# The second matrix of both MLPs by seven block products, in a pass of its own through DRAM

## The reference

```
def squared_relu_mlp(x, w1, w2):
    return jnp.square(jax.nn.relu(x @ w1)) @ w2
```

## Time and profile before

| | us |
|---|---|
| median of three runs | 5415.53 |
| fastest run | 5411.13 |
| span of the profiled execution (core 5, the slowest of 8: 5385.8 to 5402.6) | 5402.6 |
| PE busy in it | 5231.8 |
| DVE, ACT, POOL busy | 2641.7, 1955.8, 751.2 |

### The profile page before, as it was taken

One profiled execution on the slowest core, in us unless ns is written; L12 is line 12 of the kernel. 1 busy time (PEld: TensorE's weight loads), 2 busy tenths in 40 slices (PEclk: granted clock), 3 DMA queues, 4 the chain that ended last, 5 costly groups with the idle time before them and its releaser, 6 DMA issues.

```text
span 5402.6 us, 80099 instructions; the slowest of 8 cores (5385.8 to 5402.6 us)
## 1 busy us (share of the span) xinstructions
PE 5231.8 (97%) x27646; PEld 2542.2 (47%) x27646; DVE 2641.7 (49%) x4779; ACT 1955.8 (36%) x3529; POOL 751.2 (14%) x1206
## 2 busy tenths in 40 slices
PE   8999999999999989999999999999999999999997
PEld 3444444444444434444656555444444444444446
DVE  3645556665333743433554444476634337433337
ACT  3434432333222342132444555323421235223224
POOL 1111110000000300001312222000000013000013
PEclk9999999999999999999999999999999999999999
DMA  9333559876544685455642332568864557645443
GB/s 165 58 56 52 84 102 182 187 166 135 94 72 80 139 195 85 71 84 86 112 111 55 66 67 60 117 161 183 174 118 71 86 85 153 150 80 92 73 84 91
DMA packets 358732, 578.04 MB, mean 107 GB/s; under 512 B 127808, under 2 KB 197312, under 8 KB 358208
## 3 DMA queue, kind: packets, MB, share of 16 engines
q0 software_dynamic: 102816, 340.90, 40.0%
q1 hardware_dynamic: 255520, 232.02, 15.4%
HBM read 789.12 MB, written 99.61 MB: 165 GB/s over the span
## 4 chain that ended last, share of the span: by engine, by line
PE 84%; DMA 8%; DVE 3%; issue 2%; SPq 1%; ACT 1%; POOL 0%; DVEq 0%; ACTq 0%; POOLq 0%
PE bank L427 81%; DMA t<-z 4%; DVE t L443 2%; PE bank L1602 2%; DMA z<-t 1%; ACT t L440 1%; DMA x2b<-t 1%; DVE t L446 1%; DMA t<-xq 1%; SPq L230 1%; DMA t<-w2l 1%; DMA hgD<-t 1%; SPq L240 0%; DMA t<-w 0%; DMA x<-t 0%
## 5 line engine op out<-in xcount | busy, mean ns | idle before, releaser
L427 PE MATMUL bank<-t,t 128*128 128x512 bf16 (+3 forms) x25438 | 5133.6, 364 | 147.9 <-DVE t L443 51.8
L427 PEld LDWEIGHTS bank<-t,t 128*128 128x128 bf16 x25438 | 2406.5, 99 | 2793.4 <-issue 359.9
L443 DVE TENSOR_TENSOR t<-t,bank 128x512 f32<-128x512 f32 x1024 | 699.0, 686 | 1498.0 <-PE bank L427 1491.6
L440 ACT ACTIVATE t<-bank 128x512 f32<-128x512 f32 (+5 forms) x1396 | 718.4, 555 | 1707.7 <-PE bank L427 1689.3
L440 ACT ACTIVATE t<-t 128x512 f32<-128x512 f32 (+3 forms) x1208 | 747.1, 623 | 890.8 <-DVE t L443 693.1
L443 DVE TENSOR_TENSOR t<-t,t 128x512 f32<-128x512 f32 (+6 forms) x1428 | 901.1, 668 | 176.4 <-ACT t L440 76.2
L230 POOL DMA_DIRECT2D t<-w x416 | 219.8, 530 | 2503.7 <-PE bank L427 2369.3
L440 ACT ACTIVATE t<-t,t 128x512 bf16<-128x512 f32 (+5 forms) x525 | 333.6, 669 | 488.7 <-DVE t L443 355.5
L443 POOL TENSOR_TENSOR t<-t,t 128x512 f32<-128x512 f32 (+2 forms) x276 | 328.3, 1202 | 458.0 <-DVE t L443 268.9
L446 DVE SCALAR_TENSOR_TENSOR t<-t,t,t 128x512 f32<-128x512 f32 (+2 forms) x428 | 301.4, 728 | 132.1 <-DMA t<-z 77.7
L440 ACT ACTIVATE t<-bank,t 128x256 bf16<-128x256 f32 (+2 forms) x332 | 174.5, 566 | 218.2 <-PE bank L427 109.5
(11 more groups left out here) (38 smaller groups left out, 350.1 us busy)
## 6 DMA issues: line engine op xcount, KB each, us to landing
t<-w POOLq DMA_DIRECT2D x416, 512.0 KB, 7.5
t<-z SPq DMA_DIRECT2D x192, 256.0 KB, 6.1
t<-w2l POOLq DMA_DIRECT2D x116, 384.0 KB, 6.2
z<-t SPq DMA_DIRECT2D x128, 256.0 KB, 6.3
t<-w_out POOLq DMA_DIRECT2D x51, 512.0 KB, 8.7
t<-xq SPq DMA_DIRECT2D x64, 256.0 KB, 5.5
x<-t SPq DMA_DIRECT2D x64, 256.0 KB, 6.3
t<-x SPq DMA_DIRECT2D x64, 256.0 KB, 3.8
```

The costliest lines, as they stand in the source:

```text
L427: fns = [lambda e, o=o, l=l, r=r, a=a, b=b: e.matmul(out=o, lhsT=l, rhs=r, start=a, stop=b, **kw) for (o, l, r, a, b) in items]
L440: return self.P.op("act", lambda e: e.activation(out=out, in_=in_, func=func, **kw), c_act(n, bias is not None and scale is not None), **k)
L443: return self.P.op(eng, lambda e: e.tensor_tensor(out=out, in0=a, in1=b, op=op), c_pool(n) if eng == "pool" else c_dve(n, rate), **k)
```

## The change

- **Two passes.** `phase_w1` makes all hidden tiles of a layer, in 32 groups for each half, and stores them in DRAM (`hD`, 0.5 MB for each group). The order is groups 0 to 13 of half 0, then 14 to 31 of both halves with the same weights, then 0 to 13 of half 1; so w1 is read 46/32 times instead of twice. x16 and T of half 1 stand in SBUF as well, in what was the accumulators' arena (`"xB"`), and `phase_out` now stores z of s = 0, 1 in DRAM, too.
- **The second matrix by seven products.** A `Chunk` is a quarter q (16 row blocks) of the hidden features of one half: 8 loads of 0.5 MB from `hD`, and 8 DVE subtractions of 128x2048 in `Chunk.part`. `group2` multiplies it with two row blocks of outputs at a time, 8 groups of 7 products for each chunk, 7 chunks in each layer: 56 groups. The eighth (half 1, q = 3) is multiplied plainly, in four parts of 256 columns, with 16 row blocks where it was 12.
- **Its additions.** Of the seven results of a group five are added by DVE from PSUM straight into z; two (`side`) are copied by ACT into a tile of the arena `"t"` (room for two) and added into z by POOL. The products on X wait for the addition before them.
- **z.** `init` loads z from DRAM in pairs of row blocks and applies the residual's gain and bias with ACT, two groups ahead. Three of eight pairs of half 0 are stored and loaded again for LayerNorm (`ln_item`).
- **w2 in bf16.** `convert` casts w2 from DRAM to DRAM, 32 DMAs of 2 MB float32 to 1 MB bf16 for each layer, on POOL's queue: two after each `o_proj` of `phase_m` for layer 0, one after every fourth item beside attention for layer 1. The second matrix is then loaded as bf16 by SP, 128 transfers of 0.5 MB a layer.
- **LayerNorm.** The second operation of `norm_tile` and the sum of squares in `stat2` go to POOL for s = 2, 3 of `phase_out`, and so does the second operation for half 0 of the MLPs.

Counted in the built programs: matmuls of 512 columns 21564 before, 20412 after (1152 fewer); of 256 columns 2792 and 3304 (512 more).

```diff
             v_proj(p, wv, j, vv)
             o_proj(p, wo, j, so)
+            convert(k, 0, 8 * p + 2 * j, 2)
             scan(p, j, qk, vv, so, kk)
...
+def convert(k, layer, i, n):
+
+
+    after = [o for o in k.P.ops[-40:] if o.eng == "pe"][-1:]
+    for i in range(i, min(i + n, 32)):
+        j = (i // 8, i % 8)
+        k.conv[(layer,) + j] = k.P.dma("pool", k.d["w2c_%d" % layer][j], k.d["w2_%d" % layer][j], 1 << 20, extra=after)
...
+def products(k, ws_, W, last, X, banks, after, free=None):
...
+    plan = (("X", lo, 0, "B11", None), ("Z", lo, 1, "B21", ("raw", 0)), ("X", sa, 0, "T2", None), ("Y", sa, 1, "T1", ("S", 0)),
+            ("X", sb, 0, "T3", None), ("Y", sb, 1, "B22", ("S", 1)), ("X", hi, 1, "T4", ("raw", 1)))
+    for i, (bn, w, j, o, drop) in enumerate(plan):
+        first = bn not in bank
+        if first:
+            bank[bn] = P.ps(banks)
+        b, (ts, x) = bank[bn], X[o]
+        g = k.mm([(b[:], w[:, j, kp * 128:kp * 128 + 128], x(kp), first and kp == 0, kp == 7) for kp in range(8)], 8 * c_mm(512),
+                 more=not first, reads=[w] + ts, **({"writes": [b]} if first else {"rw": [b]}))
...
+        after(i, b, g)
+        if i in (1, 5, 6):
+            P.free(b)
+        paced(k, g)
...
+        stored[(pr, n)] = P.store(k.d["hD"][pr, n // 8, n % 8 // 4, :, :, n % 4].rearrange("o p t -> p o t"), hq[:], 1 << 19, reads=[hq])
...
+class Chunk:
...
+        for o in (0, 1, 3, 2):
+            for half in range(2):
+                t = self.R[(o, half)] = P.sb(2048, F16, [4, 512], ar="ops", al=True)
+                P.dma("sp", t[:], k.d["hD"][blk, q, half, o], 1 << 19, writes=[t], extra=[stored[(blk, 8 * q + 4 * half + i)] for i in range(4)])
...
+    def sub(self, o, a, b, h, **kw):
+        self.k.tt("dve", o[:], a[:], b[:], ALU.subtract, 2048, rate=2.0, **kw)
...
+    NA = 14
+    order = [(n, 0) for n in range(NA)] + [(n, p) for n in range(NA, 32) for p in range(2)] + [(n, 1) for n in range(NA)]
...
+    def init(blk, n):
+
+        for s in (2 * blk, 2 * blk + 1):
+            while k.later and not P.room(1024, F32, "acc"):
+                paced(k, None)
...
+    def group2(blk, q, n, cur, nxt):
...
+        def add(z, b):
+            k.tt("dve", z[:], z[:], b[:], ALU.add, 512, reads=[b], rw=[z])
+
+        def side(z, b):
+            t = P.sb(512, ar="t")
+            k.act(t[:], b[:], AF.Copy, 512, reads=[b], writes=[t])
+            k.tt("pool", z[:], z[:], t[:], ALU.add, 512, reads=[t], rw=[z])
             P.free(t)
...
+        def after(i, b, g):
+            if i == 1:
+                side(C[(0, 0)], b)
+            elif i == 3:
+                side(C[(1, 1)], b)
+            else:
+                add(C[{0: (0, 0), 2: (0, 1), 4: (1, 1), 5: (0, 1), 6: (1, 0)}[i]], b)
...
+    for blk, q in steps[:-1]:
+        cur = nxt
+        at = steps.index((blk, q)) + 1
+        nxt = Chunk(k, *steps[at], stored)
...
+            its = [f for i, it in enumerate(its) for f in ([it] if i % 4 else [it, lambda: convert(self.k, 1, len(self.k.conv) - 32, 1)])]
```

More of the change, by code:

```diff
@@ L938, in norm @@
             return
-        o = P.half(("x16", s), ar="x" if s < 2 else None, dt=F16)
+        ar = "x" if s < 2 else "xB"
+        o = P.half(("x16", s), ar=ar, dt=F16)
         if s < 2:
@@ L1027, in __init__ @@
         self.todo = []
-        for i, (name, idx, shape, sums) in enumerate(reqs):
+        for i in range(len(reqs)):
             self.todo += [(i, "raw", 0), (i, "raw", 1)]
-            if i and reqs[i - 1][3]:
+            if i:
                 self.todo += [(i - 1, "S", 0), (i - 1, "S", 1)]
-        if sums:
-            self.todo += [(i, "S", 0), (i, "S", 1)]
+        self.todo += [(i, "S", 0), (i, "S", 1)]
         self.ts = {}
@@ L1040, in pump @@
             i, kind, part = self.todo[0]
-            name, idx, shape, sums = self.reqs[i]
-            t = k.unit([shape[0] // 2, shape[1]], F16, until is not None)
+            t = k.unit([2, 1024], F16, until is not None)
             if t is None:
@@ new lines, in products @@
+def products(k, ws_, W, last, X, banks, after, free=None):
+    P = k.P
+    lo, hi, sa, sb = W
+    bank = {}
+    plan = (("X", lo, 0, "B11", None), ("Z", lo, 1, "B21", ("raw", 0)), ("X", sa, 0, "T2", None), ("Y", sa, 1, "T1", ("S", 0)),
[7 more added lines that the diff above has]
+                 more=not first, reads=[w] + ts, **({"writes": [b]} if first else {"rw": [b]}))
+        if drop and last:
+            ws_.drop(*drop)
+        if free:
+            free(o)
+        after(i, b, g)
+        if i in (1, 5, 6):
+            P.free(b)
+        paced(k, g)
@@ L1110, in late, with w1_ops, phase_w1 @@
+def w1_ops(x, s):
+    d = {"B11": [x[(kp, s)] for kp in range(8)], "B21": [x[(kp + 8, s)] for kp in range(8)], "B22": [x[(kp + 8, s + 1)] for kp in range(8)]}
+    for i in range(4):
+        d["T%d" % (i + 1)] = [x[("T", i, kp, s)] for kp in range(8)]
+    return {o: (ts, lambda kp, ts=ts: ts[kp][:]) for o, ts in d.items()}
+def phase_w1(k, layer, x16, ws_, order):
+    P = k.P
+    PB = [0, 1, 2, 3, 4, 5]
+    stored = {}
+    def late(*a, **kw):
         P.bias += 30
-        eng(*a, **kw)
+        k.act(*a, **kw)
@@ L1112, in late @@
         P.bias -= 30
-    def group1(h, har, n, x, ss, pops):
-        s0, s1 = ss
-        (lo, hi, sa, sb), drop = ws_.get(), ws_.drop
-        def prod(b, first, W, j, X):
-            g = k.mm([(b[:], W[:, j, kp * 128:kp * 128 + 128], X(kp)[:], first and kp == 0, kp == 7) for kp in range(8)], 8 * c_mm(512),
-                     more=not first, reads=[W] + [X(kp) for kp in range(8)], **({"writes": [b]} if first else {"rw": [b]}))
-            if pops:
-                paced(k, g)
-        def T(j):
-            return lambda kp: x[("T", j, kp)]
+    X = {0: w1_ops(x16, 0)}
@@ new lines, in phase_w1, with done @@
+    for at, (n, pr) in enumerate(order):
+        if at == 0 or order[at - 1][0] != n:
+            W = ws_.get()
+        if at == len(order) - 8:
+            (a, b), (d, e) = P.arena["w0"]
+            P.arena["w"] = [(a, b), (d, e - 8192 // GR)]
+        last = at + 1 == len(order) or order[at + 1][0] != n
+        if pr not in X:
+            while k.later:
+                paced(k, None)
+            X[pr] = w1_ops(x16, 2 * pr)
+        hq = P.sb(2048, F16, [4, 512], ar="h")
+        c = {}
+        def done(t, i, relu=True):
+            if relu:
+                late(t[:], t[:], AF.Relu, 512, rw=[t])
+            late(hq[:, i], t[:], AF.Square, 512, reads=[t], par=[hq])
+            P.free(t)
@@ new lines, in after @@
+        def after(i, b, g):
+            if i == 0:
+                c[0] = copy(b)
+            elif i == 1:
+                k.tt("dve", c[0][:], c[0][:], b[:], ALU.add, 512, reads=[b], rw=[c[0]])
+                done(c[0], 0)
+            elif i == 2:
+                c[1] = copy(b)
+            elif i == 3:
+                c[3] = copy(b)
+            elif i == 4:
+                k.tt("dve", c[3][:], c[3][:], b[:], ALU.add, 512, reads=[b], rw=[c[3]])
+                done(c[3], 3)
+            elif i == 5:
+                k.tt("dve", c[1][:], c[1][:], b[:], ALU.add, 512, reads=[b], rw=[c[1]])
+                done(c[1], 1)
+            else:
+                done(copy(b, AF.Relu), 2, False)
@@ new lines, in arena_w2 @@
+def arena_w2(k):
+    P = k.P
+    P.close()
+    n = 4096 // GR
+    w = P.arena["w0"]
+    acc = P.arena["acc"]
+    taken = {g for lo, hi in w + acc for g in range(lo, hi)}
+    ops = [g for g in range(P.low, P.ngr - n + 1, n) if not any(g + i in taken for i in range(n))][:22]
+    assert len(ops) == 22
+    taken |= {g + i for g in ops for i in range(n)}
+    (a, b), (c, d) = w
+    rest = [(d - 2 * n, d)]
+    for g in range(P.low, P.ngr):
+        if g not in taken:
+            if rest[-1][1] == g:
+                rest[-1] = (rest[-1][0], g + 1)
+            else:
+                rest.append((g, g + 1))
+    P.arena = {"w": [(a, b), (c, d - 2 * n)], "w0": w, "acc": acc, "ops": [(g, g + n) for g in ops], None: rest[1:] + [(d - n, d)], "t": [(d - 2 * n, d - n)]}
```

414 lines of the change are left out of this document (201 added, 213 removed).

## The result

The kernel before took 5410.32, 5411.13 and 5415.53 us and the changed kernel 5517.95, 5550.22 and 5554.55: a ratio of **1.024, interval 1.018 to 1.030**. Forecast were 5252 us (0.970) in a range of 5200 to 5325. In many executions the four cores of one die run at a lower clock for a time: all times and ratios here leave those executions out, and where a trace holds such a die, the other die's cores are read.

The account below looks back on a forecast made before the run. PE was taken as the bound (5231.8 of 5402.6 us busy); -192 - 28 + 11 + 6 + 20 + 8 + 6 + 6 = -163 gave a 5240 us span, plus 12.9 to the median: 5252 us, range 5200 to 5325.

Parts of the forecast that it names:

- PE's loads there are prefetched: phase_m and attention: casts delay no PE loads, only their issue holds POOL; +6 us, bounds 0 and 35.
- Rival 2: DMA: conversions hold up kD, hgD or weight loads and each MLP's front saturates; +64 us, 5316, chance 0.10.
- Additions of the second matrix: Second pass: DVE and side additions free banks nearly in time; 0.1 us for each of 112 groups, +11, bounds 0 and 56.
- rival 1: Second pass: POOL's side additions pace it, 0.7 us overrun in each of 112 groups; +67 us, 5319, chance 0.15.
- LayerNorm of half 0 beside the second matrix: Second pass: POOL's LayerNorm operations delay side additions in most of 13 groups, 10 us a layer; +20, bounds 0 and 45.
- Differences: Between chunks: 128x2048 DVE subtractions of 1.09 us delay additions, some twice a turn, 12 turns; +6, bounds 0 and 17.
- switch: From first pass to second: z loads wait for slots that x of half 1 frees late; +8, bounds 0 and 24.
- phase_out and the first groups: There more z and hD traffic brings the DMA share from 0.87 to about 1; +6, bounds 0 and 25.
- PE busy near 5040: Sign in the profile after, whole kernel; the prediction is wrong if PE busy falls by less than 185 us.
- removed matmuls are removed time: PE, full in the MLPs' steady stretches: fewer matmuls save 248.8 us, added ones cost 56.6, net -192.
- no gap above 5 us at the turn of halves: Sign in the profile after: PE has no gap above 5 us where the MLP's halves meet.
- the old turn: Between MLP halves: PE gaps of 22.3 and 6.1 us vanish, as x no longer comes from DRAM there; -28.

Follow-up runs that it names:

- experiment 1: The kernel before with the 64 DRAM to DRAM casts added at the change's places, their output unused: 5599.06 us.
- experiment 2: The change without the 64 casts, w2 read as float32 and cast in its load: 5361.86 to 5367.4 us, ratio 0.993 to the kernel before.
- experiment 6: The change with all seven additions of a second-pass group on DVE: ratio to the kernel before 1.012 with the casts, 0.979 (5286.79 and 5294.4 us) without.
- experiment 5: The change with all 64 casts moved into the first pass of the MLP that reads them: 5530.13 and 5530.53 us, ratio 1.024 to the kernel before.
- experiment 8, first kernel: The change without casts, second-pass additions, every LayerNorm's second operation and phase_out's statistics on DVE: 5307.16 and 5309.47 us, ratio 0.983 to the kernel before.

## Why the prediction was wrong

- **The step that failed: "PE's loads there are prefetched", +6 (0 to 35) for the casts.** They cost 168 to 195 us (experiments 1, 2, 6), and as much in the first pass (experiment 5). My price of a cast was right (6.4 us of the DMA engines predicted, 6.1 measured), and so was the share of 0.62 in the attention; in `phase_m` it was 0.65 where I had 0.75. I took "the engines have spare share" for "nothing waits", and looked at loads with a distance. What stands between one PE instruction and the next there is a store and a transpose (`kD`, `hgD`, `oD`; 2.7 us to landing in the median for `oD`); beside casts the worst take 27 to 80 us, and SP's own queue stops at them. Why a store or a transpose gets so late, no run here shows. Rival 2 named this, at +64: the mechanism right, its size 2.6 times too small, since I took the upper ends of terms of which the one for the casts was bounded by POOL's issue time (0.54 us each).
- The Trainium skill, DMA: Bandwidth & Descriptors, section Queues, rings and completion order, says that each DMA engine takes turns between queues by packet. By that rule a small store waits for one long piece at each turn, and shorter rows help. The runs agree in part: rows of a tenth the length gave 46 of 195 us back without the change and 77 of 168 with it; what holds up the attention's stores at short rows no run here settles.
- **"Additions of the second matrix", +11.** Taken off POOL they gave 63 and 72 us. That is rival 1 near its price (+67), with the sign that it named: gaps released by DVE, and DVE by POOL. The overrun was not one of every group, as the rival had it: those with statistics did not gain from the move (experiment 6). I set the rival too low (0.15) by a weak comparison: the two rows of POOL that differ by 8% have different output types, and DVE was busy in only half of both stretches (114.24 of 220 us, 76.42 of 160). The rule of the Trainium skill, SBUF — State Buffer, section Who interferes with whom, that a DVE instruction with two SBUF inputs and a POOL instruction that reads SBUF exclude each other, fits what was measured: 1282 against 685 ns, and 678 against 683 with one input in PSUM. From 2150 to 2250 us of the change POOL's addition took 1538 ns, and DVE's of the same shape 1114 in place of 685.
- **Rivals 1 and 2 were given as alternatives; both came true at once,** one of them much larger. A sum of the two even at their own prices (+131) would have been 5383.
- **"LayerNorm of half 0 beside the second matrix", +20, "Differences", +6, switch +8:** mis-sized. In experiment 6, with `side` gone, the second passes lose 44.6 and 31.1 us, 66 more than before, against 34 booked; how the 66 divide among the three was not measured. The switch was free: PE was busy 132.00 of 132 and 120.00 of 120 us from 1848 and from 1980 on. 128x2048 takes 1219 ns undisturbed, not 1090, and 1423 in the change.
- **phase_out and the first groups, +6:** PE lost 4, 9 and 19 us against before in 770 to 1040, 1040 to 1300 and 3600 to 3900 us (257.42, 240.38 and 271.60 against 261.50, 249.36 and 290.60): 32, above the upper bound of 25. Whether the DMA engines or LayerNorm's work there cause it was not told apart; with that work on DVE the second stretch lost 18 us instead of 9 on the core read (experiment 8, first kernel).
- **"PE busy near 5040", -192.** PE is busy 5098.0 us, 134 less and not 192, and by the prediction's own sign (a fall under 185) the step "removed matmuls are removed time" was wrong in size. Of the 58 us that are missing, 40 are the longer matmuls in the two stretches of the second pass; in experiment 6, where PE stops less often, it is busy 5069.6, which is 162 less.
- **Right:** the matmul counts; 12.09 us a group in the first pass; no gap above 5 us at the turn of halves in the second (4.17 us at most on core 3); the old turn. PE's timeline where the earlier trace rows had gaps of 7.32 and 10.57 us:

```profile
1849.79 98.36 PE L427 MATMUL bank<-t,t 128*128 128x512 bf16 x448
1948.31 12.47 PE L427 MATMUL bank<-t,t 128*128 128x512 bf16 x56 [0.16 <-DVE t L443]
```

- With the measured sizes the sum comes near: -192 - 28 + 240 (casts and `side` together, 1.024 less 0.979) + 66 + 32 = +118 us, against the 128 measured. The first term is too large by the stops above, so part of the agreement is luck.

## What to carry to other kernels

Before adding background DMA traffic, look for stores, transposes and few-buffered tiles on other queues that PE reaches through one or two steps: judge by the longest time to landing, not by share or median. In this kernel a cast that a load does anyway, hidden, was not worth a pass through DRAM. Moving LayerNorm's additions from POOL to DVE, with both inputs in SBUF, gained nothing here and may have cost 18 to 42 us; what paid was to move the additions that free a PSUM bank. And price a stop of PE by the time from group to group, since its idle time alone hides a part.

## What the hardware showed unexpectedly

- One issue of a DMA transpose on SP took 46.6 us (median 1.23) beside casts; the longest in the same stretch of the kernel before was 10.1.
- In one execution (the first of the kernel without the reload) matmuls of 512 columns averaged 683 to 918 ns by core instead of 382 to 384, with the granted clock shown as 1.00; the spans were 10,812 to 15,093 us. Other executions of the same kernel took 5291 and 5298 us. No run says why.
